# Three of four gate groups of an attention layer projected by token, and their gate turned to channels through DRAM

## What is computed

```
proj = h @ w_in
q = rms_norm_2(proj[..., :B_INNER].reshape(bsz, t, B_HEADS, B_HEAD_DIM), q_norm_w)
k = rms_norm_2(proj[..., B_INNER:2 * B_INNER].reshape(bsz, t, B_HEADS, B_HEAD_DIM), k_norm_w)
v = proj[..., 2 * B_INNER:3 * B_INNER].reshape(bsz, t, B_HEADS, B_HEAD_DIM)
z = proj[..., 3 * B_INNER:]
...
s = jnp.einsum('bchd,bmhd->bhcm', q_n, k_n).astype(jnp.float32) * scale + bias
p = jax.nn.softmax(s, axis=-1).astype(v_n.dtype)
return jnp.einsum('bhcm,bmhd->bchd', p, v_n)
...
o = (o.astype(jnp.float32) * jax.nn.silu(z.astype(jnp.float32))).astype(h.dtype)
return o @ w_out.astype(h.dtype)
```

## Time and profile before

| | |
|---|---|
| median of 3 runs (lowest, highest) | 1341.62 us (1340.92, 1343.47) |
| the profiled execution: its own time, its span | 1341.56 us, 1339.7 us |
| TensorE matmuls, share of the span | 99% |
| VectorE (DVE), ScalarE (ACT), GpSimd (POOL) | 73%, 55%, 11% |
| granted TensorE clock | 1.0 |
| read from and written to HBM | 305.67 MB, 24.13 MB |

### The profile page before, as it was taken

The page is one execution under the profiler, slowest core; times in us unless marked ns, Lnnn a source line. Parts: engine busy times, 40 slices in busy tenths (PEclk is TensorE's granted clock), DMA queues, the critical chain, the costliest instruction groups (busy, mean ns, idle before and its releaser), DMA issues.

```text
span 1339.7 us, 19604 instructions
## 1 busy us (share of the span) xinstructions
PE 1332.1 (99%) x7279; PEld 1124.8 (84%) x7279; DVE 975.6 (73%) x1309; ACT 735.9 (55%) x1096; POOL 142.3 (11%) x233
## 2 busy tenths in 40 slices
PE   9999999999999999999999999999999999999999
PEld 5445999988888888888999988888888888888887
DVE  4558999988679898999677668846667576665552
ACT  2213445555656656556688775465655646555531
POOL 0000012000001000000000100002234224201000
PEclk9999999999999999999999999999999999999999
DMA  9999999875566766586644756656878988877662
GB/s 382 396 416 365 372 347 409 325 252 190 173 234 222 229 228 221 178 272 208 195 141 155 223 185 234 190 188 212 261 227 249 276 251 267 237 222 211 199 197 83
DMA packets 86516, 328.90 MB, mean 245 GB/s; under 512 B 11088, under 2 KB 11488, under 8 KB 81952
## 3 DMA queue, kind: packets, MB, share of 16 engines
q1 hardware_dynamic: 67392, 261.30, 56.9%
q0 software_dynamic: 19040, 66.45, 16.2%
HBM read 305.67 MB, written 24.13 MB: 246 GB/s over the span
## 4 chain that ended last, share of the span: by engine, by line
PE 73%; DMA 12%; DVE 10%; issue 2%; ACT 2%; SPq 0%; POOL 0%; DVEq 0%; ACTq 0%; POOLq 0%
PE acc L838 27%; PE acc L842 14%; PE acc L781 9%; PE acc L782 9%; PE acc L783 9%; DMA mod_ring<-mod_w 7%; DVE w_lo L1784 3%; DMA raw<-weights 3%; PE misc L1094 2%; DMA gate_ring<-weights 2%; DVE mod_ring L1754 1%; DVE gate_ring L1754 1%; DMA l_x<-l_d 1%; PE misc L1084 1%; DVE mod_late L1754 1%
## 5 line engine op out<-in xcount | busy, mean ns | idle before, releaser
L1784 DVE TENSOR_TENSOR w_lo<-raw,w_hi 128x1024 fp32r<-128x1024 f32 x392 | 470.4, 1219 | 166.4 <-ACT w_hi L1258 162.0
L1258 ACT ACTIVATE w_hi<-raw 128x1024 fp32r<-128x1024 f32 x392 | 405.4, 1054 | 309.3 <-DMA raw<-weights 225.7
L838 PE MATMUL acc<-b_op,w_hi 128*128 128x512 f32 x1280 | 324.6, 395 | 0.2 <-DVE vo L1828 0.2
L838 PEld LDWEIGHTS acc<-b_op,w_hi 128*128 128x128 f32 x1280 | 230.1, 189 | 42.3 <-DVE vo L1828 0.4
L842 PEld LDWEIGHTS acc<-b_op,w_lo 128*128 128x128 f32 x1280 | 174.5, 190 | 12.9
L842 PE MATMUL acc<-b_op,w_lo 128*128 128x256 f32 x1280 | 178.3, 282 | 0.0
L781 PE MATMUL acc<-w_hi,b_op 128*128 128x512 f32 x384 | 150.1, 391 | 0.0
L782 PE MATMUL acc<-w_lo,b_op 128*128 128x512 f32 x384 | 149.5, 389 | 0.0
L783 PE MATMUL acc<-w_hi,b_op 128*128 128x512 f32 x384 | 149.4, 389 | 0.0
L838 PE MATMUL acc<-a_op,w_hi 128*128 128x512 f32 x512 | 129.0, 394 | 0.7 <-DVE a_op L1794 0.7
L838 PEld LDWEIGHTS acc<-a_op,w_hi 128*128 128x128 f32 x512 | 92.2, 189 | 17.5 <-ACT w_hi L1258 0.9
(11 more groups left out here) (297 smaller groups left out, 1929.8 us busy)
## 6 DMA issues: line engine op xcount, KB each, us to landing
raw<-weights SPq DMA_DIRECT2D x392, 512.0 KB, 4.7
mod_ring<-mod_w SPq DMA_DIRECT2D x26, 1024.0 KB, 14.7
u_ring<-weights SPq DMA_DIRECT2D x32, 512.0 KB, 14.2
gate_ring<-weights POOLq DMA_DIRECT2D x30, 512.0 KB, 8.5
mod_late<-mod_w SPq DMA_DIRECT2D x6, 1024.0 KB, 7.7
head_d<-head POOLq DMA_DIRECT2D x32, 128.0 KB, 4.1
t<-head_d POOLq DMA_DIRECT2D x32, 128.0 KB, 5.9
p_d<-p_tt POOLq DMA_DIRECT2D x16, 192.0 KB, 5.2
```

The lines of the kernel that those rows point to most:

```text
L838: nc.tensor.matmul(to, w_hi[:, slot, ch], op[:, kt], start=kt == 0, stop=False, skip_group_check=True)
L1258: nc.scalar.activation(w_hi[:, m.c % HL_SLOTS], raw[:, q.c % RAW_SLOTS], ACT.Copy).then_inc(own.up(s_hi), 1)
L1784: nc.vector.tensor_tensor(w_lo[:, slot], raw[:, q.c % RAW_SLOTS], w_hi[:, slot].bitcast(F32), ALU.subtract).then_inc(own.up(s_lo), 1)
```

## The change

The groups z0, z1 and z2 are projected by token, like q, k and v; z3 stays joined. Their weights are laid out accordingly. ACT takes the silu straight from the accumulator, scaled by the token's root, into `t1` (tokens on the partitions). DVE transposes blocks into `head_32`, POOL writes them to a DRAM tensor `z_d` and reads them back turned into `t1`, where DVE waits for them before the product with the attention's result.

```diff
+TURNS = tuple(of for of in B_ORDER if of[0] in "qk" or of in (("z", 0), ("z", 1), ("z", 2)))
...
+            def gate_turned(i):
+
+                n = turn_of("z", i)
+                pool.wait_ge(s_head_32, n)
+                to_dram(head_32[:], z_d, s_head_d)
+                pool.wait_ge(s_head_d, 64 * n)
+                from_dram(z_d, t1[:], s_z_t)
...
             for i in range(2):
                 pool.wait_ge(s_biased, i + 2)
                 bias_rows(i + 2)
+                gate_turned(i)
                 probabilities_turned(i + 1)
                 heads_turned(i + 2, 0)
                 heads_turned(i + 2, 1)
                 if i == 0:
                     residual_turned(2)
                     residual_turned(3)
+            gate_turned(2)
             probabilities_turned(3)
...
-                if kind == "z":
+                if (kind, i) == ("z", 3):
                     joined(g, b_op, fillers=b_fillers.get((kind, i)))
...
+            def gate_by_token(i):
+
+                g = group_b("z", i)
+                act.wait_ge(s_used, slab_of(Num(g + 1)).c)
+                if i:
+                    act.wait_ge(s_opnd, O_B + i)
+                to = t1[:, 0:4 * T].rearrange("p (m a c) -> p a m c", m=GM, a=2)
+                for half in range(2):
+                    of = acc[:, unit_of(g) % 2, half * GC:(half + 1) * GC].rearrange("p (m c) -> p m c", m=GM)
+                    nc.scalar.activation(to[:, half], of, ACT.Silu, scale=r_tok[:, half:half + 1]
+                                         ).then_inc(own.up(s_zb if half else s_act), 1)
...
-                    if i:
+                    if i == 3:
                         act.wait_ge(s_opnd, O_B + i)
-                    low_half(group_b("z", i), 0)
+                        low_half(group_b("z", i), 0)
                     hi_parts(n + 4, 4)
+                elif i < 3:
+                    gate_by_token(i)
+                    hi_parts(n, 2)
+                    exponentials(i + 1)
+                    hi_parts(n + 2, 5)
+                    operand_of_out(i)
+                    hi_parts(n + 7, 1)
...
-                    evicted_half(group_b("z", i), 0, r1)
+                    if i == 3:
+                        evicted_half(group_b("z", i), 0, r1)
...
+                elif i < 3:
+                    dve.wait_ge(s_zb, i + 1)
+                    dve.sem_inc(own.also(s_free), 1)
+                    dve.wait_ge(s_head_d, 64 * (turn_of("z", i) - 1))
+                    nc.vector.transpose(head_32[:], t1[:]).then_inc(own.up(s_head_32), 1)
+                    lo_parts(n, 3)
+                    probabilities(i + 1)
+                    lo_parts(n + 3, 3)
+                    dve.wait_ge(s_z_t, 64 * (i + 1))
+                    gated_values(i)
+                    lo_parts(n + 6, 1)
+                    low_of_values(i)
+                    lo_parts(n + 7, 1)
```

More of the change, by code:

```diff
@@ L68 @@
 U_B = U_AOUT + 2 * (G_B - G_AOUT)
-U_BOUT = U_B + 5 * 4
+U_BOUT = U_B + 4 * 4 + 1
 O_H = KT
@@ L150, with turn_of @@
            ("q", 3), ("k", 3), ("v", 2), ("z", 2), ("v", 3), ("z", 3))
+TURNS = tuple(of for of in B_ORDER if of[0] in "qk" or of in (("z", 0), ("z", 1), ("z", 2)))
+def turn_of(kind, i):
+    return TURNS.index((kind, i)) + 1
 def group_b(kind, i):
@@ L165, in unit_of @@
         return U_BOUT + g - G_BOUT
-    return U_B + sum(2 if kind == "z" else 1 for kind, _ in B_ORDER[:g - G_B])
+    return U_B + sum(2 if of == ("z", 3) else 1 for of in B_ORDER[:g - G_B])
 def low_of(g, h):
@@ L172, in low_of @@
         return 2 * (g - G_A) + h + 1
-    return 2 * (G_AOUT - G_A) + 2 * B_ORDER[g - G_B][1] + h + 1
+    return low_of(G_AOUT - 1, 1) + h + 1
 def first_half(g):
@@ L374, in program @@
         query_d = nc.dram_tensor("query_d", (P, HEADS * T), F32).ap()
+        z_d = nc.dram_tensor("z_d", (32, 2 * GM, 4, P), F32).ap()
         s_raw = [sem(f"s_raw{i}") for i in range(RAW_SLOTS)]
@@ L493, in program @@
         s_zb = sem("s_zb")
+        s_z_t = sem("s_z_t")
         s_y = sem("s_y")
@@ L714, in heads_turned @@
             def heads_turned(i, k):
-                n = 2 * i + k + 1
+                n = turn_of("qk"[k], i)
                 pool.wait_ge(s_head_32, n)
@@ L1679, in head_factors @@
                 if i or k:
-                    act.wait_ge(s_head_32, 2 * i + k)
+                    act.wait_ge(s_head_32, turn_of("k", i - 1) if k == 0 else turn_of("q", i))
                 head_squares(unit_of(g) % 2, 0.0 if k else log_q)
@@ L1706, in gate_b @@
             def gate_b(i):
-                act.wait_ge(s_zbr, i + 1)
+                act.wait_ge(s_zbr, 1)
                 nc.scalar.activation(t1[:, 0:4 * T], t1[:, 0:4 * T], ACT.Silu).then_inc(own.up(s_zb), 1)
+            def gate_by_token(i):
[8 more added lines that the diff above has]
+                                         ).then_inc(own.up(s_zb if half else s_act), 1)
             def operand_of_out(i):
@@ L1737, in _ @@
                     gate_b(i)
[L1738 to L1741, removed]
+                    hi_parts(n + 1, 2)
                     operand_of_out(i)
@@ L2400, in heads_scaled @@
                 if i or k:
-                    dve.wait_ge(s_head_d, 64 * (2 * i + k))
+                    dve.wait_ge(s_head_d, 64 * (turn_of("qk"[k], i) - 1))
                 nc.vector.transpose(head_32[:], t3[:]).then_inc(own.up(s_head_32), 1)
@@ L2432, in probabilities, with gated_values, low_of_values @@
                 nc.vector.transpose(p_tt[:], p_t[:]).then_inc(own.up(s_turned), 1)
+            def gated_values(i):
+                dve.wait_ge(s_pv, i + 1)
+                add(t1[:, 0:4 * T], t1[:, 0:4 * T], misc[:, 0:4 * T], ALU.mult, done=s_tmp)
+            def low_of_values(i):
+                dve.wait_ge(s_rnd, O_B + 1 + i)
+                nc.vector.tensor_tensor(a_lo[:, 4 * i:4 * i + 4], tiles(t1), a_hi[:, 4 * i:4 * i + 4].bitcast(F32),
+                                        ALU.subtract).then_inc(own.up(s_opnd), 1)
             for kind, i in B_ORDER:
@@ L2463, in _ @@
                     dve.wait_ge(s_zb, i + 1)
-                    dve.wait_ge(s_pv, i + 1)
-                    add(t1[:, 0:4 * T], t1[:, 0:4 * T], misc[:, 0:4 * T], ALU.mult, done=s_tmp)
+                    gated_values(i)
                     lo_parts(n + 2, 1)
[L2467 to L2471, removed]
+                    low_of_values(i)
                     lo_parts(n + 3, 5)
@@ L2525, in build_stream @@
         column = D * "qkvz".index(kind) + GC * j
-        b.append(joined_slabs(m, column) if kind == "z" else slabs(m, [column]))
+        b.append(joined_slabs(m, column) if (kind, j) == ("z", 3) else slabs(m, [column]))
     rest = np.concatenate([g, grp, joined_stage(i["pool_w_out"][0], quarters), joined_stage(a, order_a),
```

## The result

The changed kernel takes 1344.64 us (median of 20 executions, 1340.1 to 1348.83); the kernel before, on the same chips, 1341.2 (20 executions, 1339.57 to 1344.67). The ratio is 1.0024, 95% interval 1.0016 to 1.0031: slower by about 3.2 us. The forecast was 1340.3, range 1339.0 to 1343.8. What came is the rival "slower than before".

A forecast was written before the change was run, and what follows sets the result against it. TensorE was taken as the bound, busy 1332.1 of 1339.7 us. From 1341.56 us, 1.7 saved on three z groups gives 1339.9; 0.4 added for a short wait gives 1340.3, range 1339.0 to 1343.8.

The forecast's parts named there:

- slower than before: Rival: z0's gate lands late in DVE's wait, TensorE idles in k2; over 1344.3 us from a 1047.8 landing; chance 0.14.
- The pace of the slabs: TensorE, groups z0 to z2: by token each takes 24.39 instead of 24.95 us, 1.7 us saved in all.
- The thin place: TensorE at k2's last slab: the low part's lead over TensorE falls from 3.8 to 0.4 us.
- The chain from the landing: DVE and ACT, from z0's gate landing to k2's last slab being ready: 13.5 us, so ready at 1056.5.
- the landing that decides: z0's gate in DVE's wait: beyond 1043.4, each us later is one us of TensorE idle in k2.
- The landing of z0's gate: End of z0's turn through DRAM: the reads land at 1043.0, from 1041.7 to 1046.1.
- POOL's start of the writes: POOL's queue behind residual and bias load: z0's gate writes start at 1027.5, with 1.4 us taken off.
- the wait for the gate's writes: POOL, after issuing z0's four gate writes: 4.8 us, taken from the 4.76 behind one residual write.
- the reads: z0's gate read back from DRAM: landing 4.8 to 7.4 us after issue, median 6.1.
- two more us on each of the write and the read: In the slower rival: shared DMA engines lengthen both waits of the gate's turn, giving 1345 us.
- Contention alone: DMA engines: 1.5 MB moved each way takes room from the weights; costed at nothing while pauses cover it.
- z1 and z2: Later gates: z1 lands at 1133.9, leaving k3's last slab a 1.9 us lead; z2's wait never reaches TensorE.

The follow-up runs named there:

- e1: Changed kernel with DVE and ACT taking up z0's and z1's turned gates only behind the next q heads' scaling: 1339.27 us, 0.9988 of the kernel before.
- e2: Changed kernel with POOL turning z0's and z1's gates one residual quarter earlier: 1339.55 us, 0.9989 of the kernel before.
- e12: Changed kernel with e1 and e2 together: 1339.39 us, 0.9986 of the kernel before.
- e6: Changed kernel with z0's gate read back a second time and DVE waiting for the second read: 1351.03 us, 1.0065 of the kernel before.
- e6b: e6 run again unchanged, on the same chip as e7: 1348.3 us, 1.0062 of the kernel before.
- e7: e6 plus needless matmuls, 16 behind k2's fifth slab and 24 behind its seventh: 1353.89 us, 1.0095 of the kernel before.
- e5: Changed kernel plus 16 needless matmuls behind k2's seventh slab: 1343.88 us, 1.0024 of the kernel before.
- e4: Kernel before plus the turns' DRAM writes and reads, using constants, with only POOL waiting for them: 1341.87 us, 1.0008 of the kernel before.
- e3: Changed kernel with z0 joined again, z1 and z2 by token: 1339.66 us, 0.9987 of the kernel before.

## Why the prediction was wrong

- **The pace of the slabs** was right: 24.39 us for z1, forecast 24.39; with the waits mended, e1, e2 and e12 are 1.7 to 2.0 us under the kernel before on the same chips, forecast 1.7. The rule of the Trainium skill (TensorE: Matmul & The Clock Gate, "Back-to-back issue gap"), which the page gives for a single isolated matmul, has a fixed part of 2.5 ns each; by the prediction's estimate from it the gain would have been 0.24 us in all. The measurement does not agree.
- **The thin place** was right: the idle time is before k2's last slab. The chain from the landing was put at 13.5 us and is 14.0, in four profiles at z0's gate (changed kernel, e6, e6b, e7) and in two at z1's (e5, e7). The half microsecond is a wait that the chain left out: ACT may take the squares of q2's heads only when DVE has made the product's low part. Before, that was long done and the squares started at 1043.37, with the rounding; now ACT's rounding ends at 1048.54 + 1.04 = 1049.58, the low part at 1048.67 + 1.23 = 1049.90, and the squares start then:

```profile
1048.67 1.23 DVE L2478 TENSOR_TENSOR a_op<-t,a_op 128x1024 fp32r<-128x1024 f32 x1
```

```profile
1048.54 1.04 ACT L1278 ACTIVATE w_hi<-raw 128x1024 fp32r<-128x1024 f32 x1
1049.98 0.28 ACT L1681 ACTIVATE t<-acc 128x128 f32<-128x128 f32 x1 [0.39 <-issue]
```

With TensorE there at 1056.50, the landing that decides is 1042.5 in this profile, not 1043.4. The forecast's own central landing, 1043.0, would already have cost half a microsecond.
- **The landing of z0's gate** is the step that failed: "1043.0, from 1041.7 to 1046.1". It came at 1046.3, beyond the late end. Three terms were off. First, POOL's start of the writes, 1029.8, forecast 1027.5. The forecast took 1.4 us off because "POOL's chain behind those moves up by 1.4 us". The first residual writes were indeed issued earlier, by 2.3 us (1003.84), but the wait behind them was 8.33 instead of 6.52, so the read-back began only 0.5 earlier; the wait behind the next was 6.25 instead of 4.76. In all eight profiles with z0 by token the first of these waits is 7.3 to 8.3 us, in the four with z0 joined 6.2 to 6.8, so what was gained before it was given back in it. Second, the wait for the gate's writes, 8.54, where "I take 4.8, since the write before 6.52 lay in the fuller stretch". Third, the reads, which landed about 3.2 after the last issue, forecast 6.1, the other way; 4.8, the shortest of rows 6, is no lower bound, since in e2 the quickest of the gate's DMAs took 2.3. Together 2.3 + 3.7 - 2.8 = 3.2 us.
- **What was in that wait of 8.54 us:** from 1032.2 to 1040.7 the queue of the weights moved 1.55 MB and that of POOL's transfers 1.17, the gate's 0.5 among them; the bias rows, another 0.5 MB, had been issued just ahead, and the forecast priced only their issue. The stretch taken for the emptier one became the fuller: its DMA share went from 0.81 to 0.92. In e4, with 1.11 MB of POOL's transfers and 0.51 of weights, the wait is 5.48; in e2, where neither the bias rows nor a read-back had been issued just ahead, it is 4.37 with 0.33 and 1.02. So both the weights and POOL's own earlier transfers are in it; no run moves one of them alone, and how much each costs stays open.
- **The clock** was not in the sum at all. The wait's price was taken as its length; the profile shows 3.8 us idle and 1.8 more at half clock. With these the profiled execution adds up: 1341.56 - 1.7 - 0.4 + 3.8 + 1.8 = 1345.1, measured 1345.01. What of the 1.8 remains when the clock is kept up, e5 and e7 leave open.
- **The rival** "slower than before", 0.14, had the place, the mechanism and nearly the slope right (e6). Its point of 1344.3 was passed at a landing of 1046.3, not at the 1047.8 given, since the wait starts at 1042.5 and the clock adds to it. Its "two more us on each of the write and the read" would by its own threshold have landed at 1047.0 and given 1343.5, not 1345: the 1345 that came is no proof of that sum. The chance was too low: the central lead was 0.4 us, against terms each of which scatters by about 2 us, and nothing on the other side can give time back. A lead that near zero should have put the wait in the forecast.
- **Contention alone**, which the prediction put behind the order of the wait, is nearly nothing (e4, 1.0008 with an interval that holds 1), but what else is being transferred sets when the gate lands. Both belong to one chain: full DMA engines make the landing late, and the wait's place makes it cost.
- **z1 and z2** came as forecast in the changed kernel's profile: no wait behind either. k3's last slab had a lead of 0.3 us there, and 1.7 in e3, where no idle time lies ahead of it, forecast 1.9. It is as thin as that sounds: in the profiles of e5 and e7 TensorE waits 0.63 and 2.62 us behind z1's gate. e3, with both by token, can't be told from e1, e2 and e12.

## What to carry to other kernels

A bound engine that is fed seven slabs ahead has no slack of seven slabs: look for the smallest lead in the trace, and cost an added wait against that one. Where an engine must wait in place for a DMA chain, put the wait behind the work that the bound engine needs next, or start the chain ahead of transfers nobody is waiting for; here each of the two turned 0.24% slower into 0.11% to 0.12% faster than the kernel before. Price that chain with the transfers issued just ahead of it and beside it, and not only by their issue times. When a forecast's lead is smaller than the scatter of its terms, the wait is the forecast.

## What the runs showed of the hardware that was not expected

- An idle time of TensorE of 3.66 us was followed, 1.5 us after work had begun again, by 3.4 us at the lower clock; behind idle times of 3.43, 4.24 and 5.84 us (e6, e6b) matmuls were 0.43 us apart too, almost at once. Behind those of 0.41, 0.63 and 2.62 us (e6b, e5, e7) they were not. With matmuls that nothing needs in place of the long ones the clock stayed at 1.00 (e5, e7).
- Filling an idle time with needless matmuls kept the clock and won no time that could be measured.
- The wait of POOL for the gate's four writes of 128 KB to DRAM went from 4.37 us (e2) to 9.98 (e1). All queues together moved 1.34 MB during the one and 3.18 MB during the other, 0.31 and 0.32 MB per us; in the changed kernel it was 2.76 MB in 8.54 us, 0.32.
- The landing of a chain of DMAs behind such waits differed by 5 us between executions of one kernel (z0's product at 1052.93 in e6 and 1047.87 in e6b). The changed kernel, whose time depends on it, spread over 8.7 us in 20 executions, from 1340.1 to 1348.83; e1, e2 and e12, with the same traffic, over 3.4 to 4.0 in 11 each.
